# A folded token transform for the Fourier mixer, with conditioning products in four column strips and three weight chunks loaded first

## The reference, cut to what matters

```python
def _fourier(z, fw):
    ...
    zf = jnp.fft.fft2(zg, axes=(1, 3), norm='ortho').real.astype(z.dtype)
    return jnp.einsum('blgc,gcd->blgd', zf, fw).reshape(B, L, D_B)

def _layer(x, mod, ...):
    shift1, scale1, gate1, shift2, scale2, gate2 = jnp.split(mod, 6, axis=-1)
    h = _norm(x) * (1 + scale1) + shift1
    z = h @ w_in
    ...
    y = jnp.concatenate([_chunk_gmlp(za, a_ws, a_bs), _fourier(zb, f_w), attend(q, k, v)], axis=-1) @ w_out
    x = _affine_ln(ALPHA * x + gate1 * y, ln1_g, ln1_b)
    ...

mod_ctx = (jax.nn.silu(c_ctx) @ w_ada[l] + b_ada[l])[None, None, :]
mod_lat = (jax.nn.silu(c) @ w_ada[l] + b_ada[l])[:, None, :]
```

## Time and profile before

| what | value |
|---|---|
| median of 3 runs | 3102.55 us |
| the profiled execution | 3104.43 us, span 3102.0 us |
| PE busy | 2874.1 us, 93% of the span |
| mean granted PE clock | 0.967 of full speed |
| DMA, mean over the span | 139 GB/s |

### The profile page before, as it was taken

One profiled execution on the slowest core, in us unless ns is written; L12 is line 12 of the kernel. 1 busy time (PEld: TensorE's weight loads), 2 busy tenths in 40 slices (PEclk: granted clock), 3 DMA queues, 4 the chain that ended last, 5 costly groups with the idle time before them and its releaser, 6 DMA issues. The chain is left out here.

```text
span 3102.0 us, 51048 instructions
## 1 busy us (share of the span) xinstructions
PE 2874.1 (93%) x17132; PEld 2545.3 (82%) x17132; DVE 1849.3 (60%) x3199; ACT 1279.6 (41%) x2746; POOL 401.6 (13%) x567
## 2 busy tenths in 40 slices
PE   3899999797999999799699999999999979999997
PEld 0899999644887888587599999999999978888875
DVE  4443432262998899477788777666766643443545
ACT  3111111112887888133355565555655532121111
POOL 0000000012222222122400000000000000311312
PEclk8899999898999999899799999999999989999998
DMA  7322222367544560545364555454445435243333
GB/s 251 101 82 92 91 75 74 134 246 199 132 102 89 123 141 16 165 162 185 94 224 166 172 180 185 149 162 149 145 150 163 148 132 169 78 136 117 106 127 131
DMA packets 374228, 429.97 MB, mean 139 GB/s; under 512 B 91911, under 2 KB 270486, under 8 KB 371382
## 3 DMA queue, kind: packets, MB, share of 16 engines
q1 hardware_dynamic: 355353, 418.55, 43.5%
q10 hardware_dynamic: 18720, 9.44, 1.0%
HBM read 305.71 MB, written 124.19 MB: 139 GB/s over the span
## 5 line engine op out<-in xcount | busy, mean ns | idle before, releaser
L1978 PE MATMUL fu_alpha<-fu_h,fu_w 128*128 128x384 f32 x3168 | 577.6, 337 | 19.2 <-DVE fu_h L2204 10.6
L1978 PEld LDWEIGHTS fu_alpha<-fu_h,fu_w 128*128 128x128 f32 x3168 | 556.7, 190 | 21.4 <-issue 21.3
L2464 PE MATMUL fd_acc<-fd_w,fd_f 128*128 128x512 f32 x2376 | 546.2, 392 | 26.5 <-DVE fd_w L2492 17.1
L2464 PEld LDWEIGHTS fd_acc<-fd_w,fd_f 128*128 128x128 f32 x2376 | 447.4, 189 | 125.2 <-issue 17.8
L1978 PE MATMUL fu_beta<-fu_h,fu_w 128*128 128x384 f32 x1584 | 285.4, 334 | 1.2 <-DVE fu_h L2204 1.2
L1978 PEld LDWEIGHTS fu_beta<-fu_h,fu_w 128*128 128x128 f32 x1584 | 275.5, 188 | 1.4 <-issue 1.4
L517 PE MATMUL pj_gps<-pj_ht,w_in 128*128 128x256 f32 x2160 | 268.1, 284 | 0.0
L517 PEld LDWEIGHTS pj_gps<-pj_ht,w_in 128*128 128x128 f32 x2160 | 262.7, 192 | 1.3
L2488 DVE TENSOR_TENSOR fd_f<-fd_f_stage,fd_f 128x512 fp32r<-128x512 f32 (+1 forms) x110 | 91.4, 832 | 284.2 <-ACT fd_f L2444 284.2
L2444 ACT CAST fd_f<-fd_f_stage 128x512 fp32r<-128x512 f32 (+1 forms) x110 | 63.4, 579 | 443.9 <-PE fd_acc L2464 389.3
L2178 DVE TENSOR_TENSOR fu_w<-up_w_stage,fu_w 128x512 fp32r<-128x512 f32 x264 | 181.6, 689 | 85.8 <-ACT fu_w L2042 82.7
(11 more groups left out here) (194 smaller groups left out, 4294.2 us busy)
## 6 DMA issues: line engine op xcount, KB each, us to landing
up_w_stage<-in_w_gu_dram SPq DMA_DIRECT2D x88, 512.0 KB, 4.2
fu_w_sums<-w_gu_sums SPq DMA_DIRECT2D x132, 256.0 KB, 3.3
fd_w_stage<-in_w_down_dram SPq DMA_DIRECT2D x54, 512.0 KB, 3.6
fd_f_stage<-f_t SPq DMA_DIRECT2D x88, 256.0 KB, 2.7
at_k<-k_t SPq DMA_DIRECT2D x28, 704.0 KB, 12.7
w_gu_sums<-fu_w_sums SPq DMA_DIRECT2D x66, 256.0 KB, 4.9
fo_w<-in_w_ada_dram SPq DMA_DIRECT2D x8, 2048.0 KB, 8.8
up_w_stage<-in_w_gu_dram SPq DMA_DIRECT2D x44, 256.0 KB, 4.6
```

The lines of the kernel that those rows point to most:

```text
L1978: mm = pe.matmul(out, w[x][:, j, k, :], b[y][:, j, k, :], start=opens and (k, x, y) == (0, HI, HI), stop=(k, x, y) == (KH - 1, LO, HI), sk ...
L2464: mm = pe.matmul(acc[:, t, at], f[a][:, slot, t * P:(t + 1) * P], w[b][:, w_at(st, slot), at], start=is_step(st, 0) and (a, b) == (HI, HI) ...
```

## The change

Three things at once.

1. **Strips.** A product of a `w_ada` chunk with the two vectors is no longer 8 matmuls of 2 x 512 but 32 of 2 x 128 (`ada_chunk_product`, L90 in the changed code): the four quarters of the 512 columns go to four column strips of the PE array (`tile_position`), and come out at PSUM partitions 0, 32, 64 and 96. Bias and result follow that layout, so DVE adds in four pieces.
2. **Folded transform.** The position transform uses the symmetry of cosine and sine twice. Projection stores the second and fourth quarter of `chan_dft` in reversed order of rows (its loop over groups is unrolled for this, and one ACT copy reads its columns backwards). In the Fourier phase rows t of the four quarters are added and subtracted (`fold`), and four tables of 512 x 512 (even and odd cosines, even and odd sines, 4 MB) take the place of the one complex table (2 MB) and of the twiddles. PE has 4 units (`transform`) of 48 matmuls of 128x128 by 128x256, and for the middle row one matmul of a single row, and a few more once for the row that stands alone (`fo_mid`). Each unit yields the rows k and, by the other sign, their mirror rows, stored apart in `y_rev` in rising order; the mix phase loads those for tiles 8 to 15 and turns them round by a product with the exchange matrix in place of the transpose.
3. **Order.** The phase's first transfers are the biases and three `w_ada` chunks (three buffers now), then the transform's inputs, then the tables. PE and DVE treat those three chunks before anything of the transform.

The inputs of the fold start one row late in three of four quarters, since row 0 has no mirror: for tile i = 0 the three transfers are of 127 rows, into partitions 1 to 127.

```diff
...
+def ada_rows(tile, v):
+    return tile[v:P:P // ADA_STRIPS]
+def ada_strip(q):
+    return slice(q * (P // ADA_STRIPS), q * (P // ADA_STRIPS) + 2)
+def ada_chunk_product(pe, acc, silu, w):
+    for k in range(KT):
+        for q in range(ADA_STRIPS):
+            mm = pe.matmul(acc[ada_strip(q), 0:ADA_STRIP], silu[:, k, :], w[:, k, q * ADA_STRIP:(q + 1) * ADA_STRIP],
+                           start=k == 0, stop=k == KT - 1, tile_position=(0, q * (P // ADA_STRIPS)))
+    return mm
...
-        bias = sb("ada_bias", [2, N, ADA_COLS])
-        row = sb("ada_row", [2, N, ADA_COLS])
+        bias = sb("ada_bias", [P, N, ADA_STRIP])
+        row = sb("ada_row", [P, N, ADA_STRIP])
...
-                    for k in range(KT):
-                        mm = pe.matmul(acc[0:2, n], silu[:, k, :], wa[:, n % 2, k], start=k == 0, stop=k == KT - 1)
-                    mm.then_inc(acc_done, 1)
+                    ada_chunk_product(pe, acc[:, n], silu, wa[:, n % 2]).then_inc(acc_done, 1)
...
-                    dve.tensor_tensor(row[:, n, :], acc[0:2, n], bias[:, n, :], ALU.add).then_inc(acc_read, 1)
+                    for q in range(ADA_STRIPS):
+                        at = ada_strip(q)
+                        dve.tensor_tensor(row[at, n, :], acc[at, n, 0:ADA_STRIP], bias[at, n, :], ALU.add).then_inc(acc_read, 1)
...
-            body(0, 0, True, LAT, False)
-            with eng.Fori(0, (GROUPS - 3) // 2) as i:
-                for s in range(2):
-                    body(i * 2 + (1 + s), 1 - s, True, LAT, False)
+            for g in range(GROUPS - 2):
+                body(g, g % 2, True, LAT, False)
...
+                        at = reversed_from(g, t)
+                        sp.dma_start(chan_dft[tok(g, t) if at is None else slice(at, at + P), :], st[:, slot, :]).then_inc(st_stored[slot], 16)
...
+    SLOTS = 3
+    COS_E, COS_O, SIN_E, SIN_O = range(4)
+    SET_A, SET_C, PLUS, MINUS = range(4)
+    TERMS = ((COS_E, PLUS, 0, 0), (COS_O, MINUS, 0, 1), (SIN_E, MINUS, 1, 0), (SIN_O, PLUS, 1, 1))
...
+                def load_x(i):
+                    t = i * P
+                    p0 = 1 if i == 0 else 0
+                    sp.dma_start(x[:, i, SET_A, :], chan_dft[t:t + P, :]).then_inc(x_loaded[i], 16)
+                    sp.dma_start(x[p0:P, i, SET_C, :], chan_dft[QUARTER - 1 + t + p0:QUARTER - 1 + t + P, :]).then_inc(x_loaded[i], 16)
+                    if i == 0:
+                        sp.dma_start(x[0:1, i, SET_C, :], chan_dft[HALF_T:HALF_T + 1, :]).then_inc(x_loaded[i], 16)
+                    sp.dma_start(x[p0:P, i, PLUS, :], chan_dft[3 * QUARTER - 1 + t + p0:3 * QUARTER - 1 + t + P, :]).then_inc(x_loaded[i], 16)
+                    sp.dma_start(x[p0:P, i, MINUS, :], chan_dft[HALF_T + t + p0:HALF_T + t + P, :]).then_inc(x_loaded[i], 16)
...
+                def load_chunk(c):
+                    slot, col = c % SLOTS, (FIRST + c) * ADA_COLS
+                    if c >= SLOTS:
+                        sp.wait_ge(ada_done, c - SLOTS + 1)
+                    sp.dma_start(w[:, slot], w_cols[FIRST + c]).then_inc(w_loaded[slot], 16)
...
+                def store_rows(m):
+                    s, k = m % 2, 2 * P * m
+                    sp.wait_ge(acc_read, 2 * m + 2)
+                    for dst, sign in ((y[k:k + 2 * P, D_A:D_A + D_B], 0), (y_rev[k:k + 2 * P, :], 1)):
+                        sp.dma_start(dst.rearrange("(p j) c -> p j c", j=2),
+                                     out[:, s, sign, :].rearrange("p (j c) -> p j c", j=2)).then_inc(stored[s], 16)
...
-                    sp.dma_start(x[:, i * R:(i + 1) * R, :], xs[i]).then_inc(x_loaded[i], 16)
...
-                        sp.dma_start(table_in, dft512_in.rearrange("r (i p) m -> p r i m", p=P)).then_inc(tables_loaded, 16)
-                        load_chunk(0)
...
+                load_biases()
+                for c in range(SLOTS):
                     load_chunk(c)
...
+                for i in range(I):
+                    load_x(i)
+                for at, t in enumerate((2 * QUARTER - 1, 4 * QUARTER - 1)):
+                    sp.dma_start(ex[:, at, :], chan_dft[t:t + 1, :]).then_inc(mid_loaded, 16)
+                for n in range(4):
+                    sp.dma_start(table_raw[:, n], fold_tables[n].rearrange("(i p) k -> p i k", p=P)).then_inc(table_loaded[n], 16)
+                sp.dma_start(signs[:, :], signs_in).then_inc(signs_loaded, 16)
+                sp.dma_start(ident[:, :], ident_in).then_inc(ident_loaded, 16)
+                load_past(0)
+                for m in range(I):
+                    load_chunk(SLOTS + m)
+                    if m == 1:
+                        sp.wait_ge(f_lo, I)
+                        sp.wait_ge(patched, 1)
                         sp.dma_start(ctab, dft256_in.rearrange("r (i p) m -> p r i m", p=P)).then_inc(xc_loaded, 16)
+                        sp.wait_ge(mid_done, 1)
                         sp.dma_start(xc, chan_dft[T_LAT:T_ALL, :].rearrange("(i p) c -> p i c", p=P)).then_inc(xc_loaded, 16)
...
+                    store_rows(m)
+                    if m < PAST_TILES - 1:
+                        load_past(m + 1)
+                    store_past(m)
...
+                load_chunk(CHUNKS - 1)
...
+                def fold(i):
+                    dve.wait_ge(x_loaded[i], 80 if i == 0 else 64)
                     if i == 0:
...
+                        dve.wait_ge(zeroed, 1)
+                    for ri, op in ((0, ALU.add), (1, ALU.subtract)):
+                        for a, b in ((SET_A, PLUS), (SET_C, MINUS)):
+                            dve.tensor_tensor(part(x[:, i, a, :], ri), part(x[:, i, a, :], ri), part(x[:, i, b, :], ri), op).then_inc(once, 1)
+                    dve.wait_ge(once, 4 * i + 4)
+                    for to, op in ((PLUS, ALU.add), (MINUS, ALU.subtract)):
+                        dve.tensor_tensor(x[:, i, to, :], x[:, i, SET_A, :], x[:, i, SET_C, :], op).then_inc(folded, 1)
+                def low_folded(i):
+                    dve.wait_ge(f_hi, i + 1)
+                    dve.tensor_tensor(f[LO][:, i], x[:, i, PLUS:MINUS + 1, :], f[HI][:, i].bitcast(F32), ALU.subtract).then_inc(f_lo, 1)
...
+                for c in range(SLOTS):
                     add_bias(c)
...
+                fold(0)
+                dve.wait_ge(mid_loaded, 32)
+                dve.tensor_tensor(e512[:, :].rearrange("p (h c) -> p h c", h=2), part(ex[:, 0, :], 0), part(ex[:, 1, :], 0), ALU.add)
+                dve.wait_ge(folded, 2)
+                dve.tensor_tensor(part(x[0:1, 0, PLUS, :], 1), part(ex[:, 0, :], 1), part(ex[:, 1, :], 1), ALU.subtract).then_inc(patched, 1)
+                for i in range(1, I):
+                    fold(i)
+                    low_folded(i - 1)
+                low_folded(I - 1)
+                for n in range(4):
+                    dve.wait_ge(table_hi, n + 1)
+                    dve.tensor_tensor(table[LO][:, n], table_raw[:, n], table[HI][:, n].bitcast(F32), ALU.subtract).then_inc(table_lo, 1)
...
+                def transform(m):
+                    s = m % 2
+                    if m >= 2:
+                        pe.wait_ge(acc_read, 2 * m - 2)
+                    for n, (tab, side, ri, par) in enumerate(TERMS):
+                        if m == 0:
+                            pe.wait_ge(table_lo, tab + 1)
+                        o = acc[:, s, ri, par * 256:(par + 1) * 256]
+                        middle = tab == COS_E
+                        for i in range(I):
+                            for a, b in PASSES:
+                                mm = pe.matmul(o, table[a][:, tab, i, m * P:(m + 1) * P], part(f[b][:, i, side - PLUS, :], ri),
+                                               start=(i, a, b) == (0, HI, HI), stop=(i, a, b) == (I - 1, LO, HI) and not middle)
+                        if middle:
+                            if m == 0:
+                                pe.wait_ge(signs_loaded, 16)
+                                pe.wait_ge(patched, 1)
+                            mm = pe.matmul(o, signs[0:1, 0:P], e512[:, :], start=False, stop=True)
+                    mm.then_inc(acc_done, 1)
+                for c in range(SLOTS):
+                    ada_product(c)
+                for m in range(I):
+                    if m == 0:
+                        pe.wait_ge(f_lo, I)
+                    transform(m)
+                    if m == 0:
+                        for i in range(I):
+                            pe.matmul(mid[0:1, :], signs[:, P:P + 1], part(x[:, i, PLUS, :], 0), start=i == 0, stop=False)
+                        pe.matmul(mid[0:1, :], signs[0:1, P:P + 1], e512[:, :], start=False, stop=True).then_inc(mid_done, 1)
+                    turn_past(m)
+                    ada_product(SLOTS + m)
...
+                for c in range(SLOTS + I, CHUNKS):
+                    ada_product(c)
...
+                def load_y(t, s):
+                    if not mirrored(t):
```

(12 more changed lines are left out.)

370 lines of the change are left out of this document (156 added, 214 removed).

## The result

The changed kernel takes 3120.44 us (median of 4 runs, 3116.31 to 3122.21). The kernel before took 3102.27 us on the same chip (4 runs, 3098.46 to 3105.24). The ratio is 1.0059, with an interval from 1.0044 to 1.0075: 18 us slower, where 7 us were forecast, in the range and on the side that was given the largest chance. It is also 1.4 us above the sum's own range (3101 to 3119) and inside that of a rival, serial strips or a cold PE (3119 to 3123), so the time alone does not tell which of the two came; the trace does, further down. The profiled execution took 3121.3 us (span 3119.5), 16.9 us over that of before. PE is busy for 2812.0 us instead of 2874.1 and the mean granted clock is 0.953 instead of 0.967.

What follows compares the result with a forecast made beforehand. PE was no longer taken as late, but DMA's order: slow 127-row transfers, then a chain of chunk buffers. Fourier phase +6, modulation -1, mix +2 gave +7 on 3102.55, so 3110 us, range 3085 to 3124.

Steps and rivals of the forecast that it cites:

- the sum's own range: Whole kernel: 3101 to 3119 around 3110, with a product from 1.8 to 5 us and 5 us either way on the start.
- serial strips or a cold PE: Rival, chunk products and units: strips don't overlap, or PE stays at clock 0.50 in waits; 3119 to 3123, chance 0.27.
- the one-engine end: Fourier phase start: each 127-row transfer goes through one DMA engine, 10.3 us, 30.9 for three, holding up what is queued behind.
- T0: Fourier phase: end of the transform's first unit, forecast at 684 us (657 if the transfers are spread).
- an even spread: Rival, Fourier phase start: all or nearly all engines share the 127-row transfers; 3083 us, chance 0.17.
- three different engines: Rival, Fourier phase start: each 127-row transfer on one engine, but different ones, 10.3 instead of 30.9; 3089 us, chance 0.06.
- One sign: Profile after: some 30 us from about 623 with DMA share near 1/16, some 25 GB/s, PE and DVE idle.
- ahead of its users: Fourier phase start: transfers behind the slow three need 18 us at full rate and land before they are needed.
- The chain of chunk buffers: Fourier phase after the first unit: five chunks requested late, behind a unit's stores, landing 8.8 us after issue; PE waits.
- The 3 us set aside for a lower clock: Fourier phase after the first unit: 3 us added for two units running slower after PE waits of 2 to 3 us.
- A = 3.5: Chunk product in strips: 3.5 us, twice the ideal 1.8, against 7.03 before; bounds 1.8 and 7.4.
- -1, 0 and +2: Other phases, us: modulation -1 (strips -2.3, DVE additions +1.1), projection 0 (hidden under PE), mix +2 (float32 products, 1.9).

Runs made afterwards that it cites:

- run 1: The changed kernel with each of tile 0's three transfers of 127 rows cut into 112 and 15 rows; 3091.20 us, 0.9970 of the kernel before.
- Run 5: The changed kernel with the two transfers of the middle rows issued ahead of the three chunks; 3118.62 us, 1.0047 of the kernel before.
- run 6: The changed kernel with chunks 3 to 7 requested as early as their buffers allow; 3105.78 us, 1.0011 of the kernel before.
- Run 9: The changed kernel with a chunk product's two loops exchanged, so one column strip follows the other; 3133.26 us, 1.0109 of the kernel before.
- run 3: The kernel before with the column strips alone, in modulation and Fourier phase, transform and order as before; 3098.64 us, 0.9994 of the kernel before.

## Why the prediction was right, and which terms were mis-sized

**What is late is a transfer, not PE: shown.** The step that decided the sign was the choice of the one-engine end for three transfers of 127 rows, 30.9 us. A share of 0.07 at 25 GB/s, with 10.2, 9.8 and 10.2 us of held issues, is that price, and run 1 gives it back: 29.2 us of T0, 29 of the time. The rivals of an even spread (3083) and of three different engines (3089) are out: at 627 to 634 the first and the second have both been issued, and DMA moves 25 GB/s, not twice that; and what is left over behind the tables (679 to 682) is again one engine's. One sign was met only in part. The prediction looked for some 30 us with a share near 1/16, since all that is queued behind would stand behind; there are 20, because the other engines stand idle for as long as SP does not issue, and beside the third transfer they work again. What the change would be without this term is run 1, 3091.

**Serial strips or a cold PE: out, though 3120 lies in its range.** This rival (3119 to 3123) had two conditions. Strips that don't overlap would cost 7 us a product; they cost 1.93 to 3.6. A PE that stays at 0.50 would need 10.2 us a unit behind a wait; the two units that follow the waits of 5.76 and 2.96 us and their products end 6.95 and 6.91 us after they start, the one without a wait 6.67. (The first unit takes 10.5 us, but it goes table by table behind DVE and ends 2.3 us after the last table.) What carried the time into that range are the terms below: a wait for two small rows, and chunks that land late. So the side and the main cost came as forecast; that the number lies between 3110 and the end of the range at 3124 is those terms' doing, and partly made up by luck behind the phase.

**Start to T0: 684 forecast, 693.35 measured, and the 9.35 have three parts.** The folding began at 656.80 instead of 654 (1.0 of the 2.8 is the later start of the phase). DVE then waited 5.94 us for the two middle rows: the sum had taken everything behind the slow three as "ahead of its users" at the full rate, and had not seen that SP's issue is held up by each slow transfer; the two small rows went out at 655.22, behind all seventeen transfers of the inputs. Run 5 takes this wait away and T0 by 5.9. The rest of DVE's chain took 30.6 us, against the 30 of the sum; in it the low part of a table took 2.9 us with GpSimd at work beside it, where the sum had 2.3 (2.39 in the row that it names) and 1.3 in all for GpSimd.

**T0 to the end of the phase: 62 forecast, 68.05 measured.** The chain of chunk buffers was named, and the waits of PE are there, but they sum to 18.0 us instead of some 10. The mis-sized term is the landing of a chunk: 8.8 us by the earlier trace rows, and 10.6, 10.8, 11.8 and 11.7 here. Two of these landings follow each other in the chain, those of chunk 5 (2.0 us more) and of the last (3.4 more than its 8.3). Chunk 5 was also asked for 9.6 us after the end of unit 1 instead of 6.3, since SP's issue of the values ahead of it took 3.30 us (711.06). So the last chunk lands 59.0 us after T0 (693.35) instead of 51.2. The 3 us set aside for a lower clock were in place of part of it. Why a chunk lands later than before is not shown. That this chain costs what it does is shown by run 6, which removes it. Run 9 shows its other side: longer products vanish in these waits.

**A = 3.5 for a product was right for a reason that I did not have.** At the full clock it is 1.93, close to the ideal 1.8; in the products behind waits of 5.6 and 5.8 us for a chunk the clock stands at 0.50 (1.2 GHz), and they take 3.60; behind 3.0 and 3.7 us it is 0.56 and 0.55 over the product, which takes 3.3 and 3.4. The 2.38 times of the Trainium skill ("TensorE: Matmul & The Clock Gate", section "Measured speedup vs the span model") is for three strips; here four give 3.0 times against the same matmuls strip by strip (run 9) and 3.6 times against the wide ones of before.

**Modulation, projection and mix.** The forecast was -1, 0 and +2. Modulation gave -0.25, though the DMA engines are now full where they had 2.3 us of room; the sixteen additions of DVE at the end, 286 ns each (median), take part of it and where the rest stays is open. Projection took 1.2 us more here, and in the profiles of all eleven runs the Fourier phase began at 603.7 to 605.5 instead of 602.2; run 3, whose projection phase is that of before, has 603.9, so the unrolled loop is not shown to be the cause. The +2 of the mix phase was not seen: the exchange products are there (32 records, 5.3 us), but the rest of the kernel came out 4.0 us shorter than before, which lies in the scatter of 8 us between profiles of equal code (run 3, whose code there is that of before, has 2356.0 instead of 2362.1). It cannot be settled by this measure.

**The sum.** 746 was forecast for the end of the phase (745 with the -1 of modulation) and 761.4 came: 9.35 + 6.05. The kernel ended only 10 us above the forecast because the part behind it was some 6 us shorter than the sum had it, by no merit of the sum: that is luck.
